# Two transformer blocks in fp32 on one core: up-projections with both activation halves in one 512-column matmul

## The reference, cut to what matters

```
def conv_ffn(h, w_up, conv_w, conv_b, w_down):            # first block
    up = h @ w_up                                         # 256x2048 @ 2048x11264
    up_p = jnp.pad(up, ((0, 0), (CONV_WIDTH - 1, 0), (0, 0)))
    c = conv_b + sum(conv_w[j] * up_p[:, j:j + S] for j in range(CONV_WIDTH))
    gate, val = jnp.split(c, 2, axis=-1)
    return (jax.nn.silu(gate) * val) @ w_down             # 256x5632 @ 5632x2048

def conv_ffn_2(h, w_up, ffn_conv_w, w_down):              # second block, no bias
    u = causal_dwconv3(h @ w_up, ffn_conv_w)
    g, val = jnp.split(u, 2, axis=-1)
    return (jax.nn.silu(g) * val) @ w_down
```

## Time and profile before

| | us |
|---|---|
| median of 3 runs | 2320.91 (2320.79 to 2322.02) |
| the profiled execution, whole | 2321.84 |
| its span, first to last instruction | 2320.1 |
| TensorE busy in it | 2271.1 (98%) |
| VectorE busy | 1592.2 (69%) |
| ScalarE busy | 1097.6 (47%) |
| first up-projection, about | 381 to 890 |
| second up-projection, about | 1559 to 2071 |

### The profile page before, as it was taken

How to read it: one execution, slowest core, us unless ns; L and a number is a source line. 1 busy time by engine, 2 the same in 40 slices (tenths; PEclk the granted TensorE clock), 3 DMA queues, 4 the chain that set the end, 5 groups by cost and what they waited for, 6 DMA issues and landing times.

```text
span 2320.1 us, 38263 instructions
## 1 busy us (share of the span) xinstructions
PE 2271.1 (98%) x15284; PEld 2102.0 (91%) x15284; DVE 1592.2 (69%) x1802; ACT 1097.6 (47%) x1319; POOL 147.4 (6%) x71
## 2 busy tenths in 40 slices
PE   7999999999999999999899999979999999999998
PEld 7889888999999998888898999769999999998886
DVE  5679678777887657667755766778885656565555
ACT  5454544544444444444535454544444444444444
POOL 0005100000000000000000110000000100010000
PEclk9999999999999999999999999989999999999999
DMA  8657376777787556778475454657875555555553
GB/s 304 221 174 243 127 282 232 286 285 255 262 296 274 182 184 240 285 273 311 169 244 181 147 164 159 241 199 254 290 284 187 182 182 182 183 181 198 197 190 117
DMA packets 190439, 512.98 MB, mean 221 GB/s; under 512 B 12201, under 2 KB 14201, under 8 KB 166409
## 3 DMA queue, kind: packets, MB, share of 16 engines
q1 hardware_dynamic: 190169, 511.51, 63.2%
q10 hardware_dynamic: 176, 0.14, 0.0%
HBM read 509.52 MB, written 2.10 MB: 221 GB/s over the span
## 4 chain that ended last, share of the span: by engine, by line
PE 94%; DVE 3%; ACT 1%; issue 0%; DMA 0%; POOL 0%; DVEq 0%; ACTq 0%
PE ps L1541 31%; PE ps L1542 30%; PE ps L1543 30%; DVE w_lo L916 1%; PE ps L1662 1%; PE ps L1829 1%; DVE region L1017 0%; ACT w_hi L486 0%; DVE region L1110 0%; PE ps L1884 0%; ACT region L562 0%; DVE x L1434 0%; DMA region<-in_attn_norm_g 0%; PE ps L1746 0%; PE ps L1710 0%
## 5 line engine op out<-in xcount | busy, mean ns | idle before, releaser
L916 DVE TENSOR_TENSOR w_lo<-raw,w_hi 128x1024 fp32r<-128x1024 f32 x768 | 997.3, 1307 | 663.5 <-ACT w_hi L486 658.0
L486 ACT ACTIVATE w_hi<-raw 128x1024 fp32r<-128x1024 f32 x768 | 810.2, 1059 | 1077.4 <-PE ps L1543 1014.8
L1541 PE MATMUL ps<-a_hi,w_hi 128*128 128x256 f32 x3616 | 1026.7, 284 | 2.6 <-DVE w_lo L916 1.6
L1542 PE MATMUL ps<-a_lo,w_hi 128*128 128x256 f32 x3616 | 1023.5, 283 | 0.0
L1543 PE MATMUL ps<-a_hi,w_lo 128*128 128x256 f32 x3616 | 1023.3, 283 | 0.0
L1541 PEld LDWEIGHTS ps<-a_hi,w_hi 128*128 128x128 f32 x3616 | 692.5, 192 | 4.8 <-DVE w_lo L916 2.6
L1542 PEld LDWEIGHTS ps<-a_lo,w_hi 128*128 128x128 f32 x3616 | 692.4, 191 | 0.6 <-issue 0.2
L1543 PEld LDWEIGHTS ps<-a_hi,w_lo 128*128 128x128 f32 x3616 | 692.3, 191 | 0.3
L1541 PE MATMUL ps<-w_hi,a_hi 128*128 128x512 f32 x1280 | 501.2, 392 | 2.2 <-DVE a_lo L1030 2.2
L1542 PE MATMUL ps<-w_lo,a_hi 128*128 128x512 f32 x1280 | 498.2, 389 | 0.0
L1543 PE MATMUL ps<-w_hi,a_lo 128*128 128x512 f32 x1280 | 498.1, 389 | 0.0
(11 more groups left out here) (181 smaller groups left out, 673.3 us busy)
## 6 DMA issues: line engine op xcount, KB each, us to landing
raw<-in_w_up SPq DMA_DIRECT2D x176, 1024.0 KB, 5.1
raw<-in_w_mod SPq DMA_DIRECT2D x96, 1024.0 KB, 5.2
raw<-in_w_in SPq DMA_DIRECT2D x88, 1024.0 KB, 5.1
raw<-in_w_down SPq DMA_DIRECT2D x88, 1024.0 KB, 5.0
raw<-in_w_out SPq DMA_DIRECT2D x32, 1024.0 KB, 5.1
x<-in_x SPq DMA_DIRECT2D x2, 1024.0 KB, 6.4
out_x<-x SPq DMA_DIRECT2D x4, 512.0 KB, 2.7
c_row<-in_c SPq DMA_DIRECT2D x1, 1024.0 KB, 12.4
```

The lines of the kernel that those rows point to most:

```text
L486: nc.scalar.activation(w_hi[:, hh % HL_SLOTS, :], raw[:, n % RAW_SLOTS, half * HALF:(half + 1) * HALF], ACT.Copy).then_inc(hi_ready, 1)
L916: v.tensor_tensor(w_lo[:, hh % HL_SLOTS, :], raw[:, n % RAW_SLOTS, half * HALF:(half + 1) * HALF], w_hi[:, hh % HL_SLOTS, :].bitcast(F32), ...
L1541: mmul(dst, lhs_hi, rhs_hi, start=start, stop=False, skip_group_check=True)
L1542: mmul(dst, lhs_hi, rhs_lo, start=False, stop=False, skip_group_check=True)
```

## The change

In the up-projections `a_hi` and `a_lo` lie next to each other in one tile `a_hl` (128 x 16 x 2 x 256), and one matmul of 512 columns multiplies a `w_hi` tile with both. A second one of 256 columns adds `w_lo * a_hi` on to the half that holds the product with `a_lo`. So a block now fills four banks (`quad(0)` or `quad(1)`), in each bank 256 columns of `hi*hi` and 256 of the two small products. ScalarE copies the small halves to SBUF (`up_low`, L607 of the changed kernel), VectorE adds the others out of PSUM to them (`up_sum`, L1079), and then the taps run as before, but read `up_sum` in SBUF (L624, L1096). TensorE may start the block after next once `up_sum` is there, instead of after the taps. In the programs of both engines the eviction takes the place that the taps had, and the taps come one chunk later. Since a block uses four banks, the norm's transposes in front of an up-projection have four banks instead of five (four tiles ahead, four after the first chunk); `down` begins with all of j = 0 and 1 for tokens 0 to 127, and then those for tokens 128 to 255; and the row of gate weights of the second block (`gate_row(1)`), which uses the `side` banks, moves from pair 4's value block to its gate block.

More of the change, by code:

```diff
@@ L500, in lead, with pairs @@
                     round_half(PH[name].m0 + h // 2, h % 2)
-            def pairs(name, epi, narrow=0, between=None, late=None):
+            def pairs(name, epi, narrow=0, between=None, late=None, evict=None):
                 ph = PH[name]
@@ L617, in down @@
                 lead(name, range(3))
+                evict_prev()
+                lead(name, range(3, 4))
                 epi_prev()
-                lead(name, range(3, 4))
                 for j in range(2, 4):
@@ L770, in _ @@
             norm(1, "up1", {1: 2, 3: 3})
-            pairs("up1", epi_conv(1, 0), late=gate_silu)
-            down("down1", 0, lambda: last_epi("up1", epi_conv(1, 0)))
+            pairs("up1", epi_conv(1, 0), late=gate_silu, evict=evict_conv(0))
+            down("down1", 0, lambda: last_epi("up1", evict_conv(0)), lambda: last_epi("up1", epi_conv(1, 0)))
             lead("in2", range(2))
@@ L880, in last_row @@
             def last_row(at):
-                if at == 39:
+                if at == 35:
                     gate_row(1)
-            pairs("up2", epi_conv(2, 1), between=last_row, late=gate_silu)
-            down("down2", 1, lambda: last_epi("up2", epi_conv(2, 1)))
+            pairs("up2", epi_conv(2, 1), between=last_row, late=gate_silu, evict=evict_conv(1))
+            down("down2", 1, lambda: last_epi("up2", evict_conv(1)), lambda: last_epi("up2", epi_conv(2, 1)))
             load_table(3)
@@ L942, in mod_chunk, with pairs @@
                                     ALU.add).then_inc(sem("modc_ready"), 1)
-            def pairs(name, epi, narrow=0, between=None):
+            def pairs(name, epi, narrow=0, between=None, evict=None):
                 ph = PH[name]
@@ L1062, in epi_conv, with down @@
                 return epi
-            def down(name, q, epi_prev):
+            def down(name, q, evict_prev, epi_prev):
                 ph = PH[name]
@@ L1440, in last_row @@
             def last_row(at):
-                if at == 36:
+                if at == 33:
                     gate_diag(colB(B_FPOST, KT), 80)
-            pairs("up2", epi_conv(2, 1), between=last_row)
-            down("down2", 1, lambda: last_epi("up2", epi_conv(2, 1)))
+            pairs("up2", epi_conv(2, 1), between=last_row, evict=evict_conv(1))
+            down("down2", 1, lambda: last_epi("up2", evict_conv(1)), lambda: last_epi("up2", epi_conv(2, 1)))
             dve.wait_ge(sem("row_ready"), 2)
@@ L1593, in body @@
                                 kts = [KC * K_ORDER[name][c] + 2 * half + kk for kk in range(2)]
-                                (half_T if layout == "T" else half_W)(
-                                    main(blk), hh, kts, c + half == 0, c == BLOCK_CHUNKS - 1 and half == 1).then_inc(w_used, 1)
+                                {"T": half_T, "W": half_W, "M": half_M}[layout](
+                                    quad(blk) if layout == "M" else main(blk), hh, kts, c + half == 0, c == BLOCK_CHUNKS - 1 and half == 1).then_inc(w_used, 1)
                             if between:
@@ L1789, in _ @@
             pairs("out1")
-            norm(1, range(0, 5))
+            norm(1, range(0, 4))
             def later_tiles(at):
                 if at == 0:
-                    norm(1, range(5, 8))
-            pairs("up1", between=later_tiles)
+                    norm(1, range(4, 8))
+            pairs("up1", between=later_tiles, summed=0)
             down("down1", 0, 1)
```

76 lines of the change are left out of this document (48 added, 28 removed).

## The result

The change makes the kernel slower. The median is **2339.49 us** (2336.34 to 2341.22, 4 runs) against 2321.47 us of the kernel before (2320.79 to 2322.91, 4 runs): ratio 1.0075, 95% interval [1.0058, 1.0093]. That is under 1%, but the two sets of runs are 13 us apart. The prediction said 2306, with nothing above 2317 in its range and 0.13 on this side. The profiled execution has a span of 2338.4 us against 2320.1.

The account below looks back on a forecast made before the run. TensorE's matmul stream was taken as the bound (94% of the span). 37.5 - 15.7 - 4.7 - 2.0 = 15.1 us less gave a median of 2306 us; main case's range 2297 to 2316, overall 2290 to 2317.

Parts of the forecast that it names:

- The gain of the matmuls: On TensorE in the up-projections: one matmul less per weight tile saves 0.0133 us, 37.5 us in all, 1.71 per pair.
- The ring: In pairs with w_mod, VectorE waits twice for ScalarE's taps and rounding: 46.16 us against TensorE's 44.37; chance 0.62.
- The start of an up-projection: Four banks for the norm's transposes make the third chunk 1.9 us late: 2.35 off the gain, twice, 4.7.
- hidden ring: Rival for pairs with w_mod: VectorE's waits cost TensorE nothing, so 31 us less, 2290; chance 0.18.
- the transfers: Rival in pairs with w_mod: later landings for c = 6 delay ScalarE and VectorE; 2331 at 2.4 us longer; chance 0.13.
- The side "slower": Whole-kernel outcome slower by more than about 0.2% (4.6 us); chance 0.13, all from later transfer landings.
- the term of 15.7 us given back: Pairs with w_mod exceed TensorE's need: 7 pairs by 1.8 us, 3 by 1.1.
- GpSimd's hold: In pairs with w_mod, GpSimd's multiply holds the VectorE operation behind a w_mod operation for about 1.1 us.
- Taps on VectorE: In pairs with w_mod, 16 VectorE taps from SBUF at 0.393 us each, 6.3 together.
- Hand-overs: From VectorE's addition (1.14 us) to ScalarE's taps, a hand-over of 0.15 us, twice a pair.
- TensorE's first two halves: At a pair's start, 2 x 2.77 us; with release and ScalarE's rounding of c = 2's second half, 6.66.
- The range: Whole-kernel time of 2297 to 2316 us for the main case, a microsecond per pair counting about 11 in all.

Follow-up runs that it names:

- The small product: Changed kernel with GpSimd's product of gate and value cut to 8 of 256 columns, the rest constant; 2315.24 us.
- the best version: Changed kernel with VectorE's addition and taps each one chunk earlier, and two 512-column matmuls followed by their two 256-column ones; 2294.81 us.
- two and two: Changed kernel with VectorE's addition one chunk earlier, and two 512-column matmuls then their two 256-column ones; 2299.20 us.
- four and four: Changed kernel with VectorE's addition and taps one chunk earlier, and four 512-column matmuls then their four 256-column ones; 2301.71 us.

## Why the prediction was wrong

**What held.** The gain of the matmuls: pairs without w_mod at 44.36 us, at 0.3467 us a tile. The ring and its place: VectorE's two idles, 3.3 us where 3.17 was forecast, TensorE waiting at a pair's start for a subtraction. The start of an up-projection: chunk three begins at 398.09 us, against the forecast 396.4 and 1.87 us by which this execution was already late before it (378.57 against 376.70 in the earlier trace rows). The clear rivals fell: no hidden ring, and the transfers took part in only one of the ten long pairs, with 0.84 us. The side "slower", 0.13, came true by its sign alone: it was there for the transfers.

**The step that failed** is the size of the ring, the term of 15.7 us given back: 46.16 us for a pair in the prediction's walk, 48.5 on the chip, and 43.9 us given back. By its own terms:
- *GpSimd's hold, 1.1 us forecast, 2.2 measured.* The prediction let the w_mod operation run "through" beside the product, as if the product ran too. In the traces of these pairs the product instead waits for VectorE's operation to end and only then holds the next one for its full time. In the row at 649.02 above, VectorE's w_mod operation ended at 650.96 and the product at 653.29, 2.33 us later. The earlier trace rows had it already: the product of 3.21 us ended at 674.54, and the two subtractions beside it took 4.56 us where two alone take 2.35, so 2.2 more. The 3.21 us were some 0.9 of waiting and 2.3 of work; the prediction took all of it for work that the operation ahead would cover in part. The small product took 2.1 us out of the pair.
- *Taps on VectorE, 0.393 forecast, 0.424 measured* (671.20 to the next operation at 674.59, eight in 3.39 us). They cost the same as out of PSUM: 478 ns mean here, 474 in the experiment whose taps read PSUM. A tap is no dearer than the four of the earlier trace rows: it starts 0.395 us behind the one before it in both. But the eight are two groups of four, the second waits for the first (`conv_second`), and that step is 0.62 us, before the change as after it. So the earlier trace rows differ by a wait, which the prediction took for the price of a PSUM source. 16 taps: 0.5 us.
- *Hand-overs.* From the start of the addition to ScalarE's taps 1.44 us (664.41 to 665.85) instead of 1.14 + 0.15: twice 0.15.
- *TensorE's first two halves.* After its start at 580.30 ScalarE's second rounding can begin at 586.26, so 5.96 us with the release instead of 5.6: the first matmul after a stop is slow (0.34 us to the next instead of 0.23), and the halves come 2.83 us apart, which is the slow pace. 0.4 us.

46.16 + 1.1 + 0.5 + 0.3 + 0.4 = 48.46; measured 48.51 to 48.59 in the pairs without another loss. Four misses, all in one direction, are multiplied by ten pairs, which exceed TensorE's need by 43.9 us (34.3 + 9.6) instead of 15.7.

**A term that was missing.** After some of its stops TensorE's clock falls. The timeline of TensorE in the changed kernel:

```profile
678.94 0.50 PE L1624 MATMUL ps<-a_hl,w_hi 128*128 128x512 f32 x1 [2.05 <-DVE w_lo L944]
...
680.53 0.63 PE L1624 MATMUL ps<-a_hl,w_hi 128*128 128x512 f32 x1
680.96 0.41 PE L1626 MATMUL ps<-a_hl,w_lo 128*128 128x256 f32 x1
681.17 0.63 PE L1624 MATMUL ps<-a_hl,w_hi 128*128 128x512 f32 x1
...
683.73 0.42 PE L1624 MATMUL ps<-a_hl,w_hi 128*128 128x512 f32 x1
```

After an idle of 2.05 us and four tiles at the usual pace, matmuls start 0.43 and 0.21 us apart, twice the usual, so at 1.2 GHz, until 683.73. Five tiles in 3.2 us cost 1.5 us more; that is the difference of 50.1 to 48.55, and the windows show 0.97 there. It happened in three pairs (the three windows of 0.97 above), so some 5 us of the 43.9. After the idle of 2.04 us ahead of 628.87 the matmuls were slow from the first on. The length of the stop alone does not decide it: ahead of 531.82 and 729.07 TensorE was idle for 2.08 and 2.05 us, and no matmul behind them was slow. What decides it is not settled by these rows. In the longest pair, 51.10 us, the drop and the 0.84 us of VectorE's idle for a landing come together.

**The rule of the Trainium skill** (TensorE: Matmul & The Clock Gate, Back-to-back issue gap), which that section gives for single matmuls and not for a stream with a weight load before each, would have had 7 us on TensorE if taken for this stream. The matmuls gave 1.49 us a pair in the best version (46.08 - 44.59), 33 in all, so the rows were right to go by, with the reserve that the mixed stream in its first order has a second pace. The one on operand sources (VectorE: DVE Perf Modes, The TRN2 errata), SBUF cheaper than PSUM by 62 cycles on VectorE, does not show here: 478 ns against 474. For ScalarE it has SBUF dearer by 52 cycles, 0.043 us, and the trace agrees: four taps take 1.99 us (665.85 to 667.84) against 1.81 out of PSUM.

**Closing the books.** Up to the first up-projection the changed kernel lost 1.9 us that I can't assign. First up- and down-projection: forecast -2.9, measured +19.8. Second: forecast -12.2, measured -3.4. Sum +18.3 against -15.1, and of the 33.4 between them 28.2 lie in the ten long pairs. Of the rest about 2.4 lie in the first pairs of the two up-projections, which came out 1.7 and 2.0 us longer than before instead of 0.6, and 1.9 ahead of the first. From the last matmuls of an up-projection to the end of the down-projection the changed kernel lost 1.0 and 1.8 us, against the forecast 1 each.

**The odds.** The range treated a microsecond in the ring as 11 us but gave the ring's sum only one of error. A walk of some forty durations through four engines, each read from a row where the work lay alone, leaves out the waits between them, and missed upwards. The side "slower" was tied to transfers alone; it should have held the ring itself at two microseconds more.

## What to carry to other kernels

When a change puts a wait for another engine into an in-order queue, look at what stands behind that wait. Here 32 us hung on one chunk's difference in where VectorE adds, or 24 on where ScalarE does its taps, with no work saved: let the result be ready a chunk before its reader comes to it. A ring summed from rows of work that lay alone came out too short here, since the hand-overs, holds and restarts that such rows leave out all added; give its sum a range of its own, on the far side above all. And when one program's runs spread over 14 us, look at the distance of its matmuls, stretch by stretch: here an order of them took the spread away.

## What the runs showed of the hardware

- Two paces of one stream: 512 and 256 columns by turns into the same bank take 0.347 or 0.353 us a tile, and change from one to the other only across a break of the stream; two and two 0.3484 (44.59 / 128); four and four 0.3508.
- A GpSimd multiplication of 128x1024 with two SBUF sources waits for VectorE, then holds VectorE's next operation for 2.1 to 2.2 us; here it is not hidden beside VectorE at all. How long it waits differs. In the changed kernel it was one operation (4.27 us in all); in the best version it let three go first, until 491.08, and then held the next two subtractions to 4.57 us (6.55 us in all, in the row at 486.88).
- VectorE's taps cost 0.42 us from SBUF as from PSUM: 0.39 from start to start, and 0.62 where a group of four waits for the one before.
- TensorE dropped to 1.2 GHz for 3.2 to 3.6 us behind three of its stops (2.04, 2.05 and 2.63 us) and not behind others as long (2.05 and 2.08).
